# A gated recurrence on one core: two of its seven decay levels taken from the gates themselves, and seven sum steps per pair of heads in place of nine

## What is computed

```
f = lb + (1 - lb) * sigmoid(f_raw);  logf = log(f);  k = 1 - f
a = cumsum(logf)
inter  = (q * exp(a)) @ s0
scores = sum over channels of q[t] * k[s] * exp(a[t] - a[s]), s <= t
out    = inter + scores @ v
```

## Time and profile before

| | before |
|---|---|
| median of 3 runs | 2833.1 us (2832.56 to 2836.18) |
| the profiled execution | 2830.94 us, its span 2829.2 us |
| TensorE busy | 2784.4 us, 98% of the span |
| VectorE busy | 1998.3 us, 71% |
| ScalarE busy | 1376.4 us, 49% |
| GpSimd busy | 146.9 us, 5% |
| recurrence, first sum step to last output part | 1815.3 to 1913.6 us |

### The profile page before, as it was taken

One profiled execution on the slowest core, in us unless ns is written; L12 is line 12 of the kernel. 1 busy time (PEld: TensorE's weight loads), 2 busy tenths in 40 slices (PEclk: granted clock), 3 DMA queues, 4 the chain that ended last, 5 costly groups with the idle time before them and its releaser, 6 DMA issues.

```text
span 2829.2 us, 34510 instructions
## 1 busy us (share of the span) xinstructions
PE 2784.4 (98%) x12945; PEld 2316.1 (82%) x12945; DVE 1998.3 (71%) x2267; ACT 1376.4 (49%) x1719; POOL 146.9 (5%) x109
## 2 busy tenths in 40 slices
PE   9999999999999999999999999999989999999998
PEld 7887888888888888787888888888878888888887
DVE  5666877899997676766785488687975467744555
ACT  5446454444443455547544445754554444344443
POOL 0000010010000100000000001000001001010010
PEclk9999999999999999999999999999999999999999
DMA  7963888888888777655666666408856588775664
GB/s 250 215 202 110 281 278 266 279 275 285 287 275 310 256 246 237 201 191 170 205 191 198 199 183 184 133 2 292 311 193 180 192 272 277 256 205 187 193 186 156
DMA packets 332636, 623.09 MB, mean 220 GB/s; under 512 B 36999, under 2 KB 38663, under 8 KB 330759
## 3 DMA queue, kind: packets, MB, share of 16 engines
q1 hardware_dynamic: 323543, 601.52, 67.2%
q10 hardware_dynamic: 8944, 19.56, 2.0%
HBM read 614.68 MB, written 7.27 MB: 220 GB/s over the span
## 4 chain that ended last, share of the span: by engine, by line
PE 92%; DVE 3%; DMA 2%; issue 1%; ACT 1%; SPq 0%; POOL 0%; DVEq 0%; ACTq 0%; POOLq 0%
PE ps L1398 85%; PE ps L1377 1%; PE ps L1609 1%; PE ps L1810 1%; DMA raw<-w_in 1%; PE ps L1790 1%; DMA raw<-w_o 1%; DVE wlo L1933 1%; PE ps L1419 1%; PE ps L1828 1%; PE ps L1531 0%; ACT whi L706 0%; PE ps L1511 0%; DVE macc L2137 0%; PE ps L1665 0%
## 5 line engine op out<-in xcount | busy, mean ns | idle before, releaser
L1933 DVE TENSOR_TENSOR wlo<-raw,whi 128x1024 fp32r<-128x1024 f32 x940 | 1169.0, 1249 | 730.0 <-ACT whi L706 725.2
L706 ACT ACTIVATE whi<-raw 128x1024 fp32r<-128x1024 f32 x940 | 996.2, 1061 | 1227.5 <-PE ps L1398 1118.4
L1398 PE MATMUL ps<-whi,hhi 128*128 128x512 f32 x2032 | 549.7, 392 | 4.9 <-issue 3.8
L1398 PE MATMUL ps<-whi,hlo 128*128 128x512 f32 x2032 | 545.2, 390 | 0.0
L1398 PE MATMUL ps<-wlo,hhi 128*128 128x512 f32 x2032 | 543.6, 389 | 0.0
L1398 PEld LDWEIGHTS ps<-wlo,hhi 128*128 128x128 f32 x2032 | 381.8, 188 | 79.7
L1398 PEld LDWEIGHTS ps<-whi,hlo 128*128 128x128 f32 x2032 | 381.4, 188 | 79.6
L1398 PEld LDWEIGHTS ps<-whi,hhi 128*128 128x128 f32 x2032 | 378.1, 188 | 83.2 <-issue 6.0
L1398 PE MATMUL ps<-whi,xhi 128*128 128x512 f32 x1632 | 441.3, 392 | 1.6 <-issue 1.6
L1398 PE MATMUL ps<-whi,xlo 128*128 128x512 f32 x1632 | 439.2, 391 | 0.0
L1398 PE MATMUL ps<-wlo,xhi 128*128 128x512 f32 x1632 | 436.9, 389 | 0.0
(11 more groups left out here) (311 smaller groups left out, 1479.3 us busy)
## 6 DMA issues: line engine op xcount, KB each, us to landing
raw<-w_in SPq DMA_DIRECT2D x296, 512.0 KB, 4.4
raw<-mlp_w SPq DMA_DIRECT2D x256, 512.0 KB, 4.2
mraw<-w_mod SPq DMA_DIRECT2D x384, 256.0 KB, 5.0
raw<-w_up SPq DMA_DIRECT2D x128, 512.0 KB, 4.5
raw<-w_down SPq DMA_DIRECT2D x128, 512.0 KB, 5.1
raw<-w_o SPq DMA_DIRECT2D x32, 512.0 KB, 5.6
raw<-w_ple_gate SPq DMA_DIRECT2D x32, 512.0 KB, 3.9
raw<-w_out SPq DMA_DIRECT2D x32, 512.0 KB, 5.5
```

Of the source, the lines that this page charges most:

```text
L706: nc.scalar.activation(whi[:, s % NSLOT], raw[:, s % NSLOT], ACT.Copy).then_inc(hi_done, 1)
L1398: ins = nc.tensor.matmul(ps[:, bank(par) + th], a[:, kt, th * P:(th + 1) * P], b[:, (s + u) % NSLOT, k], start=(kt == 0 and m == 0), stop= ...
L1933: nc.vector.tensor_tensor(wlo[:, s % NSLOT], raw[:, s % NSLOT], whi[:, s % NSLOT].bitcast(F32), ALU.subtract)\
```

## The change

Decays inside blocks of two and four tokens are one gate or a product of two, so the levels 1 and 2 need no sums and no exp. `LEVELS[:SUMMED]`, with `SUMMED` = 5, keep their sums; the score steps become diag, 1, 2, 64, 32, 16, 8, 4, cross. There are three units per pair (the third holds level 4 and cross), so `N_E` is 7, and `dec` alternates over the run of all units. The matrices `sums` shrink from 20 to 16 planes. The gates themselves are transposed, both directions interleaved in `fT[.., T, 2]`, and the keys appear as f - 1 where they are used (`scalar_tensor_tensor` with -1.0); the sign is taken out in `qT` and `S0`. GpSimd's `keys` is gone. The orders on TensorE and ScalarE are written anew.

```diff
-N_SUMS = 2 * (len(LEVELS) - 1) + 8
+SUMMED = 5
+N_SUMS = 2 * (SUMMED - 1) + 8
...
-        kT = [at("kT0", [P, 2, 2, T], F32, tcol_at), at("kT1", [P, 2, 2, T], F32, hhi_at + 10 * K)]
+        fT = [at("fT0", [P, 2, T, 2], F32, tcol_at), at("fT1", [P, 2, T, 2], F32, hhi_at + 10 * K)]
...
-        ESTEPS = [("level", u, h) for u in range(4) for h in range(2)] + [("init", 0, 0)]
-        SSTEPS = ["diag"] + LEVELS + ["cross"]
+        N_U = 3
+        ESTEPS = [("level", u, h) for u in range(N_U) for h in range(2)] + [("init", 0, 0)]
+        SSTEPS = ["diag", 1, 2] + LEVELS[:SUMMED] + ["cross"]
...
-                dst = qT[pair % 2][:] if j == 0 else kT[pair % 2][:, j - 1]
+                dst = qT[pair % 2][:] if j == 0 else fT[pair % 2][:, :, :, j - 1]
...
-                        before = (pair, u - 2) if u >= 2 else (pair - 1, u + 2)
-                        act.wait_ge(qk_done, before[0] * N_S + 2 * before[1] + 3)
+                        before = divmod(N_U * pair + u - 2, N_U)
+                        act.wait_ge(qk_done, before[0] * N_S + 2 * before[1] + 5)
...
                 more = pair + 1 < NPAIR
                 if more:
                     turned_rows(pair + 1, 0)
+                    turned_rows(pair + 1, 1)
                 exp_step(pair, 4)
-                if more:
-                    turned_rows(pair + 1, 1)
-                exp_step(pair, 5)
                 if more:
                     turned_rows(pair + 1, 2)
                     forget_high(pair + 1)
-                exp_step(pair, 6)
-                exp_step(pair, 7)
+                exp_step(pair, 5)
                 if pair == 0:
                     log_forget(1)
-                exp_step(pair, 8)
+                exp_step(pair, 6)
...
                 score_step(pair, 1)
-                sums_step(pair, 4)
                 if more:
                     row_turn(pair + 1, 1)
                 score_step(pair, 2)
-                sums_step(pair, 5)
+                sums_step(pair, 4)
                 if more:
                     row_turn(pair + 1, 2)
                 score_step(pair, 3)
-                sums_step(pair, 6)
+                sums_step(pair, 5)
                 if pair:
                     out_part(pair - 1, 0)
                 score_step(pair, 4)
-                sums_step(pair, 7)
                 if pair:
                     out_part(pair - 1, 1)
+                score_step(pair, 5)
+                sums_step(pair, 6)
+                if pair:
                     out_part(pair - 1, 2)
-                score_step(pair, 5)
+                score_step(pair, 6)
                 if pair:
                     out_part(pair - 1, 3)
-                sums_step(pair, 8)
-                score_step(pair, 6)
...
+                if kind == 1:
+                    if pair == 0:
+                        dve.wait_ge(pe_done, plan["pw"][0])
+                    twos = lambda x: x.rearrange("p h (i s) -> p (h i) s", s=2)
+                    nc.vector.tensor_scalar(twos(kD[:, b]), gates(0, 2, 3), -1.0, None, ALU.add)
+                    nc.vector.tensor_tensor(twos(qD[:, b]), twos(q[:]), gates(1, 2, 1), ALU.mult).then_inc(qk_done, 1)
+                    return
+                if kind == 2:
+                    fours = lambda x: x.rearrange("p h (i s) -> p (h i) s", s=4)
+                    kd, qd = fours(kD[:, b]), fours(qD[:, b])
+                    nc.vector.tensor_scalar(kd[:, :, 1:3], gates(2, 4, 3), -1.0, None, ALU.add)
+                    nc.vector.scalar_tensor_tensor(out=kd[:, :, 0:4:3], in0=gates(0, 4, 7), scalar=-1.0, in1=gates(2, 4, 3), op0=ALU.add, op1=ALU.mult)
+                    nc.vector.tensor_tensor(qd[:, :, 1:3], fours(q[:])[:, :, 1:3], gates(3, 4, 1), ALU.mult)
+                    dve.wait_ge(qk_done, m)
+                    nc.vector.tensor_tensor(qd[:, :, 0:4:3], fours(qD[:, 1 - b])[:, :, 0:4:3], gates(3, 4, 1), ALU.mult).then_inc(qk_done, 1)
+                    return
...
-                nc.vector.tensor_tensor(blocks(kD[:, b]), keys, decays(0), ALU.mult)
+                for side in range(2):
+                    keys = bass.AP(f, side * (2 * kind + 1), [[4 * T, P], [4 * kind, width // kind], [2, kind]])
+                    nc.vector.scalar_tensor_tensor(out=blocks(kD[:, b])[:, :, side], in0=keys, scalar=-1.0, in1=decays(0)[:, :, side],
+                                                   op0=ALU.add, op1=ALU.mult)
...
-            def keys(hg):
-                for d in range(2):
-                    pool.wait_ge(lf_done, 2 * hg + d + 1)
-                    f = rows5[:, RF + d, :, hg * GW:(hg + 1) * GW]
-                    nc.gpsimd.tensor_scalar(f, f, -1.0, 1.0, ALU.mult, ALU.add).then_inc(k_done, 1)
```

More of the change, by code:

```diff
@@ L105, in shape_constants @@
     sums = []
-    for a in range(0, len(LEVELS) - 1, 2):
+    for a in range(0, SUMMED - 1, 2):
         for d in range(2):
@@ L110, in shape_constants @@
         for th in range(TH):
-            sums += [split[-1][d], cross[th]]
+            sums += [split[SUMMED - 1][d], cross[th]]
     s, tt = j, q
@@ L1205, in exp_step @@
                     elif h == 0:
-                        before = (pair, u - 2) if u >= 2 else (pair - 1, u + 2)
-                        act.wait_ge(qk_done, before[0] * N_S + 2 * before[1] + 3)
+                        before = divmod(N_U * pair + u - 2, N_U)
+                        act.wait_ge(qk_done, before[0] * N_S + 2 * before[1] + 5)
                     src = ps[:, b:b + 2].rearrange("p t (l c) -> p t l c", c=P // 2)
-                    dst = dec[u % 2][:].rearrange("p l r k c -> p k (l r) c")[:, 2 * h:2 * h + 2]
+                    dst = dec[(N_U * pair + u) % 2][:].rearrange("p l r k c -> p k (l r) c")[:, 2 * h:2 * h + 2]
                 else:
@@ L1749, in row_turn @@
                 if j:
-                    pe.wait_ge(k_done, 2 * (pair // 2) + j)
+                    pe.wait_ge(x_f, 4)
                 row = (RQ, RF, RF + 1)[j]
@@ L2434, in decay_step, with gates @@
                     dve.wait_ge(far_done, pair)
-                q, k = qT[pair % 2], kT[pair % 2]
+                q, f = qT[pair % 2], fT[pair % 2]
+                def gates(first, block, second):
+                    return bass.AP(f, first, [[4 * T, P], [2 * block, 2 * T // block], [second, 2]])
                 if kind == "diag":
                     dve.wait_ge(kt_done, 3 * pair + 3)
-                    nc.vector.tensor_tensor(kD[:, b], k[:, 0], k[:, 1], ALU.add).then_inc(qk_done, 1)
+                    nc.vector.scalar_tensor_tensor(out=kD[:, b], in0=f[:, :, :, 0], scalar=-2.0, in1=f[:, :, :, 1], op0=ALU.add, op1=ALU.add)\
+                        .then_inc(qk_done, 1)
+                    return
[14 more added lines that the diff above has]
+                    nc.vector.tensor_tensor(qd[:, :, 0:4:3], fours(qD[:, 1 - b])[:, :, 0:4:3], gates(3, 4, 1), ALU.mult).then_inc(qk_done, 1)
                     return
@@ L2441, in decay_step @@
                 dve.wait_ge(d_done, pair * N_E + 2 * u + 2)
-                e = dec[u % 2]
+                e = dec[(N_U * pair + u) % 2]
                 if kind == "cross":
@@ L2448, in decay_step @@
                         planes = (lambda t: halves[:, :, t, 0:4:3]) if d == 0 else (lambda t: halves[:, :, t, 1:3])
-                        nc.vector.tensor_tensor(two(kD[:, b, :, far]), two(k[:, d, :, far]), planes(d), ALU.mult)
+                        for hh in range(2):
+                            nc.vector.scalar_tensor_tensor(out=two(kD[:, b, :, far])[:, hh], in0=two(f[:, :, far, d])[:, hh], scalar=-1.0,
+                                                           in1=planes(d)[:, hh], op0=ALU.add, op1=ALU.mult)
                         ins = nc.vector.tensor_tensor(two(qD[:, b, :, near]), two(q[:, :, near]), planes(1 - d), ALU.mult)
@@ L2456, in decay_step @@
                 blocks = lambda x: x.rearrange("p h (b s i) -> p (h b) s i", s=2, i=kind)
-                keys = bass.AP(k, 0, [[4 * T, P], [2 * kind, width // kind], [2 * T + kind, 2], [1, kind]])
-                nc.vector.tensor_tensor(blocks(kD[:, b]), keys, decays(0), ALU.mult)
+                for side in range(2):
+                    keys = bass.AP(f, side * (2 * kind + 1), [[4 * T, P], [4 * kind, width // kind], [2, kind]])
+                    nc.vector.scalar_tensor_tensor(out=blocks(kD[:, b])[:, :, side], in0=keys, scalar=-1.0, in1=decays(0)[:, :, side],
+                                                   op0=ALU.add, op1=ALU.mult)
+                if j == 3:
+                    dve.wait_ge(qk_done, m)
                 nc.vector.tensor_tensor(blocks(qD[:, b]), blocks(q[:]), decays(2), ALU.mult).then_inc(qk_done, 1)
```

14 lines of the change are left out of this document (6 added, 8 removed).

## The result

| | before | after |
|---|---|---|
| median of 5 runs each | 2832.56 us (2831.61 to 2836.18) | 2844.22 us (2843.55 to 2846.71) |
| the profiled execution | 2830.94 us, span 2829.2 | 2844.22 us, span 2842.4 |
| mean granted clock | 0.996 | 0.992 |

The ratio after to before is 1.0044, 95% interval [1.0033, 1.0056]: slower by 11.7 us at the median, where 6.9 was forecast. TensorE has 7.6 us less to do, and the recurrence takes 13 us more.

What follows compares the result with a forecast made beforehand. In the recurrence TensorE and VectorE run close together and wait for each other by turns. Walked waits +4.4 and lower clock +2.5 give +6.9 us on 2833.1, so 2840.0; range 2836.0 to 2847.0.

Steps and rivals of the forecast that it cites:

- two new waits: Pair 2: unit 2's exp step awaits decay 4, squares delay cross; TensorE rests 1.9 and 0.6 us.
- longer rest at row turn 1: Pair 2: TensorE has only score step 1 and a turn before it, resting 2.7 us instead of 1.6.
- The removed work: Two level sum steps in each of four pairs, 7.6 us of TensorE; GpSimd's keys, 0.85 us in pair 0.
- The rival in which it comes through: Recurrence: the new waits find slack, TensorE leads, 7.6 + 0.85 us come off: 2824.6; chance 0.05.
- I take the plain price: VectorE decay steps: gates read with gaps cost as plain ones, decay step 2 being 4 x 0.34 = 1.36 us.
- the rival of the slow reads: Decay steps 2, 4, 5 and cross: gaps cost up to 0.34 us more per doubled instruction; 2844; chance 0.13.
- The rule on VectorE's modes: One-source float32 instructions give two results a cycle; the four `tensor_scalar` on the chain would make the sum 0.5 us smaller.
- the falls: New rests in pairs 0 to 2 could halve the clock, costing 0 to 4.8 us; 2.5 taken.
- in pair 0 VectorE leads and hides most of it: Clock term: in pair 0 VectorE hides most of a fall's cost, up to 1.6 us per fall.
- Read strictly: Skill's clock page: clock falls after the array stood idle; charges pair 0's rest alone, sum some 5 us.
- the wider reading: Clock falls though TensorE wasn't idle throughout, as before 1908; rests in pairs 0 to 2 count, 2.5 us taken.
- the waits less the removed work: Walk of pairs 0 to 3 in the new order: +0.3, +1.6, +2.2, +0.3, together +4.4 us.

Runs made afterwards that it cites:

- run of three moves: Changed kernel with third copy and forget_high before unit 2's exp step, first_queries behind decay step 1, squares' sum one keep step later: 2825.68 us, ratio 0.9983.
- cheap decay step 2: Changed kernel with the three reorderings on ScalarE and VectorE, plus decay step 2 on plain halves (computes something else in level 2): 2822.18 us, ratio 0.9964.
- plain step: Changed kernel with decay step 2 reading and writing plain halves, no gaps (computes something else in level 2): 2839.37 us, ratio 1.0029.
- idle products: Changed kernel with unread TensorE products, 11 behind score step 1 in pairs 1 and 2, 13 behind score step 4 in pair 0: 2841.98 us, ratio 1.0035.
- second run with idle products: The changed kernel with the same 11 and 13 unread TensorE products, measured again: 2841.31 us, ratio 1.0033.
- single moves: Changed kernel with one reordering each: third copy and forget_high earlier 2836.54 us; squares' sum later 2840.67; first_queries earlier 2838.47.

## Why the prediction was right, and where its sizes were off

**Direction and mechanism: right.** 2844.22 lies in the range 2836.0 to 2847.0, 4.2 us above the 2840.0. The forecast said that two new waits and a longer rest at row turn 1 would take back what TensorE was spared, and each showed with its size: the rest ahead of score step 5 in pair 0 was 4.0 us (3.8 forecast), forget_low waited 2.4 in pair 0 and up to 2.1 later (some 2), out_mean_squares up to 1.9 (1.9), and the turn up to 3.3 (2.7). Taking each away by itself gave 7.7, 3.6 and 5.8 us, and all three together 18.5. That is shown, not argued. Of its other signs, the rest ahead of score step 5 in pair 2 was 1.95 (2 forecast) and the clock stood at 0.50 for some us in pair 0. The end of score step 0 of pair 3 came 27.5 us behind that of pair 2, where 25 was forecast, and the half-size instructions of decay step 2 took 0.61, where 0.42 was. That the total lies in the range owes something to the range's breadth: pair 0, forecast to grow by 0.3 us, grew by 3.5, the largest miss.

**The removed work: its size was right, its share of the final gain is not shown.** The rival in which it comes through (2824.6) named the condition, slack at the two new waits. The run of three moves made that slack by order alone and came to 2825.68; with a cheap decay step 2 the recurrence was 8.5 us shorter, 7.3 of them TensorE's work. But the kernel before has rests as well, 3.3 us at the row turns of pairs 1 and 2, which an earlier first_queries might shorten. The three moves were never put into it, so what they would give without the change stays open.

**Decay step 2: its size failed.** The step of the prediction that failed is "I take the plain price": 4 x 0.34 = 1.36 us. It was 1.90, 0.54 more in each of four pairs, 2.2 us if it is on the chain in each. The plain step shortened laps 1 and 2 and, with the three moves, every lap; in pair 0 of the changed kernel the low clock took its gain back. No row read such gates; that excluded a gain, but it was no argument that the price sits at that end. Two tokens taken out of each four (two elements out of eight in fT, two out of four in the others) cost 0.61 for 0.42 (45% more, not double), while a level step, which takes every second element of fT, cost what was priced: two instructions of 417 ns and the product, 1.27 for 1.28. So the rival of the slow reads had the right mechanism, at one kind of step of those that it named, and with half the doubling.

**The rule on VectorE's modes.** Instructions with one source and gaps: 0.39 us for the 256 elements of decay step 2, 0.42 for the 512 of decay step 1 (two out of each four elements of fT), where a product of 512 takes 0.69; 256 plain ones took 0.28, 0.20 by the spacing of starts. The section "Mode 2×_2P — use both read ports for one tensor" of the Trainium skill's page "VectorE: DVE Perf Modes" asks nothing of the strides inside; the rows at 0.20 plain and at 0.42 for 512 agree, but the one in decay step 2 cost 0.31 by spacing, where the rule knows no such step. By that rule the whole decay step would have been 0.13 shorter than my 1.36; the gaps made it 0.54 longer. The rule spoke of one instruction in four, and the other three took 0.52 to 0.54 by spacing for my 0.34.

**The clock: its size failed.** I took 2.5 us for the falls. Read from the laps with and without idle products they cost 2.2, 1.2 and 1.2 in pairs 0 to 2. In pair 3 a score step at the low level took 2.09 where it had taken 1.17, 0.9 more, read from one trace each; in the second run with idle products, none of them in pair 3, it took 1.17 again. Together 5.5 in the profiled execution. The step that failed is "in pair 0 VectorE leads and hides most of it": score step 5, the init sum and score step 6 stood at the half clock right behind the rest, at 2.07, 1.60 and 1.81 for 1.16, 0.84 and 1.04, 2.4 us, and of those 2.2 came through to the lap. In this stretch VectorE itself waited, 0.28 us for score step 5 and 1.44 for score step 6. The fall in pair 3 stood in no term.

The clock fell behind rests of 4.01 us in pair 0, 3.26 in pair 1 and 3.27 in pair 2, but also behind one of 2.03 us in the second run with idle products. The Trainium skill's page "TensorE: Matmul & The Clock Gate", section "What's actually happening", has the clock fall after the array has stood idle. Read strictly it charged pair 0's rest alone; this trace has pairs 1 and 2 charged as well, so the wider reading, the one taken from the earlier trace rows, was the right one, and I then charged it too little.

**The sum.** The clock's 5.5 and decay step 2's 2.2 leave 5.7 of the 13.4 us by which the four pairs grew. The forecast had 4.4 for this, the waits less the removed work, and no run measures that term alone; the other 1.3, some 0.3 a pair, I have not traced. The medians grew by 11.7. One thing stays open: the idle products gave 2.2 and 2.9 us by the medians, and 4.6 in the laps of a trace. Falls that come in some executions only, as the one behind 2.03 us, would explain the difference, but two traces can't settle it; the mean clocks of the 11 executions, 0.994 to 0.996, fit it and prove nothing.

## What to carry to other kernels

Work removed from the busiest engine paid here only when the order behind it was rewritten for the shorter lap. So list, for each engine, which instruction now waits for something later than before, and what stands behind it in its queue. Here three calls moved by a few places turned 11.7 us lost into over 5 gained. A rest made on TensorE costs twice, once for itself and again for the slow steps behind it, so a forecast should charge the fall for rests like these (in the changed kernel and under the single moves each one of 3.26 to 4.01 us was followed by the half clock), also where another engine seems to lead. And when a reordering turns a loss into a gain, put it into the old kernel too, or its share of the gain stays unknown.

## What the runs showed that I had not expected

- The gaps of decay step 2 (two elements out of eight in fT, two out of four in kD, qD and qT) cost VectorE 0.61 instead of 0.42 us per product of 128 x 256; every second element cost nothing measurable (417 ns), nor did two out of four at one source alone (0.69 us for 512).
- A product of float32 of 128 columns is two pieces in the trace and takes 0.22 us; half of that is no count for filling a rest.
- ScalarE's copies into the interleaved fT take 630 ns, those into the plain kT 596: 0.03 us more for a write to every second element.
- The clock's fall isn't a function of the rest just ahead of it. Behind 2.03 us it fell in one execution and not in another of the same kernel; with the plain decay step 2 it fell behind the turn's rest of 2.58 us in pair 1 and not behind 2.57 in pair 2; the last output parts took 3.81 us behind a rest of 2.46 and 5.44 behind one of 2.48, with the same products.
